# Four taps of a recurrent branch's convolution moved to ScalarE and GpSimd, and three taps of a 31-tap convolution moved from TensorE to VectorE

## The reference, cut to what matters

```python
h = x @ w_in + b_in                      # 1024 -> 2048 columns
a_val, a_gate, b_gate, b_rec = ...       # four slices of 512 channels
ya = silu(layer_norm(causal_depthwise_conv(a_val * sigmoid(a_gate), conv_w, conv_b), ...))   # 31 taps
r  = causal_depthwise_conv(b_rec, lru_conv_w, lru_conv_b)                                     # 4 taps
gate_r = sigmoid(r @ w_a + b_a)          # block-diagonal products
gate_i = sigmoid(r @ w_x + b_x)
a  = exp(-8 * gate_r * softplus(-lam))
u  = sqrt(1 - a*a) * (gate_i * r)
yb = scan(h = a*h + u) * gelu(b_gate)
y  = concat([ya, yb]) @ w_out
```

## Time and profile before

| | |
|---|---|
| median of 3 runs | 3682.91 us (3682.41 to 3684.94) |
| the profiled execution | 3684.21 us, span 3682.3 us |
| busy over the whole span | PE 96%, PEld 77%, DVE 49%, ACT 33%, POOL 15% |
| the stage of the change | from the start to about 260 us |

### The profile page before, as it was taken

How to read it: one execution, slowest core, us unless ns; L and a number is a source line. 1 busy time by engine, 2 the same in 40 slices (tenths; PEclk the granted TensorE clock), 3 DMA queues, 4 the chain that set the end, 5 groups by cost and what they waited for, 6 DMA issues and landing times. The chain is left out here.

```text
span 3682.3 us, 41723 instructions
## 1 busy us (share of the span) xinstructions
PE 3540.3 (96%) x16052; PEld 2841.6 (77%) x16052; DVE 1788.0 (49%) x2304; ACT 1225.3 (33%) x1791; POOL 537.3 (15%) x304
## 2 busy tenths in 40 slices
PE   8989999999998999999999999999987799999997
PEld 6757888888876777767888888888876678888886
DVE  7986423223245666667423233554565674323235
ACT  4244411111134444455311112445353442212133
POOL 0015200000043000013100000445022630000004
PEclk9999999999999999999999999999987899999998
DMA  2002213122122111112222122222220122111112
GB/s 103 34 35 75 92 63 108 46 76 90 45 75 86 47 40 46 40 58 75 87 74 91 46 97 102 93 92 94 91 89 32 70 86 95 48 46 51 45 58 98
DMA packets 77471, 259.07 MB, mean 70 GB/s; under 512 B 10288, under 2 KB 11696, under 8 KB 77360
## 3 DMA queue, kind: packets, MB, share of 16 engines
q1 hardware_dynamic: 77360, 257.59, 20.8%
HBM read 244.45 MB, written 4.72 MB: 68 GB/s over the span
## 5 line engine op out<-in xcount | busy, mean ns | idle before, releaser
L202 PE MATMUL ps<-xh,whi 128*128 128x512 f32 x2768 | 964.6, 395 | 41.8 <-DVE wlo L185 18.1
L202 PE MATMUL ps<-xl,whi 128*128 128x512 f32 x2768 | 957.1, 392 | 0.0
L202 PE MATMUL ps<-xh,wlo 128*128 128x512 f32 x2768 | 956.3, 391 | 0.0
L185 DVE TENSOR_TENSOR wlo<-stage,whi 128x1024 fp32r<-128x1024 f32 (+1 forms) x361 | 505.6, 1401 | 481.3 <-ACT whi L178 480.2
L178 ACT ACTIVATE whi<-stage 128x1024 fp32r<-128x1024 f32 (+1 forms) x361 | 377.7, 1046 | 1031.8 <-PE ps L202 1003.5
L202 PEld LDWEIGHTS ps<-xh,whi 128*128 128x128 f32 x2768 | 524.1, 189 | 159.9 <-issue 28.8
L202 PEld LDWEIGHTS ps<-xh,wlo 128*128 128x128 f32 x2768 | 524.0, 189 | 110.4
L202 PEld LDWEIGHTS ps<-xl,whi 128*128 128x128 f32 x2768 | 524.2, 189 | 107.7
L202 PE MATMUL ps<-hh,whi 128*128 128x512 f32 x1216 | 422.5, 396 | 5.9 <-ACT lam_t L2272 3.9
L202 PE MATMUL ps<-hl,whi 128*128 128x512 f32 x1216 | 421.4, 395 | 0.0
L202 PE MATMUL ps<-hh,wlo 128*128 128x512 f32 x1216 | 421.1, 395 | 0.0
(11 more groups left out here) (411 smaller groups left out, 3933.1 us busy)
## 6 DMA issues: line engine op xcount, KB each, us to landing
stage<-in_w_ff SPq DMA_DIRECT2D x88, 512.0 KB, 3.4
stage<-in_w_gate SPq DMA_DIRECT2D x59, 512.0 KB, 3.2
stage<-in_w_up SPq DMA_DIRECT2D x59, 512.0 KB, 3.2
stage<-in_w_in SPq DMA_DIRECT2D x50, 512.0 KB, 3.2
ada<-in_w_ada SPq DMA_DIRECT2D x48, 512.0 KB, 3.3
stage<-in_w_qkv SPq DMA_DIRECT2D x43, 512.0 KB, 3.2
stage<-in_w_down SPq DMA_DIRECT2D x48, 448.0 KB, 3.3
stage<-in_w_out SPq DMA_DIRECT2D x24, 512.0 KB, 3.2
```

The source lines that it names most:

```text
L185: dve.tensor_tensor(wlo[slot][:, n], stage[slot][:, n], whi[slot][:, n].bitcast(F32), ALU.subtract).then_inc(w_split, 1)
L202: done = pe.matmul(acc[:, h * HALF:(h + 1) * HALF], wt[slot][:, w], xt[:, b, h * HALF:(h + 1) * HALF], start=b == 0 and wt is whi and xt i ...
```

## The change

PE_TAPS falls from 6 to 3, so DVE has 28 (in the last block 20) convolution taps to do instead of 25 (17). The recurrent branch's four taps leave DVE. ACT now writes the four products into rec, g_i, g_r and gel (L662 of the changed kernel), which are free at that time, and POOL adds them: rec+g_i, g_r+gel, and, after a wait for both, rec+g_r. PE waits for the last of these before the gate products. ACT waits for the first two additions before it overwrites gel with the gelu.

```diff
-    PE_TAPS, LATE_TAPS = 6, 8
+    PE_TAPS, LATE_TAPS = 3, 8
...
+    LRU_STEPS = 2 * LRU_TAPS - 1
+    lru_parts = (rec, g_i, g_r, gel)
...
         def _(pool):
             pool.memset(w_gates[:], 0.0).then_inc(wg_zero, 1)
+            for i in range(AB):
+                pool.wait_ge(lru_taps, LRU_STEPS * i + LRU_TAPS)
+                pool.tensor_tensor(rec[:], rec[:], g_i[:], ALU.add).then_inc(lru_taps, 1)
+                pool.tensor_tensor(g_r[:], g_r[:], gel[:], ALU.add).then_inc(lru_taps, 1)
+                pool.wait_ge(lru_taps, LRU_STEPS * i + LRU_TAPS + 2)
+                pool.tensor_tensor(rec[:], rec[:], g_r[:], ALU.add).then_inc(lru_taps, 1)
...
-                pe.wait_ge(lru_taps, LRU_TAPS * i + LRU_TAPS)
+                pe.wait_ge(lru_taps, LRU_STEPS * i + LRU_STEPS)
...
                     act.wait_ge(tap_mm, i + 1)
                     diagonals(i + 1, CONV_TAPS - PE_TAPS, PE_TAPS, diag)
+                act.wait_ge(acc_free, u + 5)
+                for t, part in enumerate(lru_parts):
+                    act.activation(part[:], r_pad[:, t:t + S], ACT.Identity, scale=col("lru_w", LRU_TAPS * i + t),
+                                   bias=col("lru_b", i) if t == 0 else 0.0).then_inc(lru_taps, 1)
+                act.wait_ge(lru_taps, LRU_STEPS * i + LRU_TAPS + 2)
                 act.wait_ge(mm_done, u + 6)
...
-                for t in range(LRU_TAPS):
-                    lru_tap(t)
-                    conv_steps(1)
                 conv_steps(min(SPLIT_AT, n_taps + 1) - step[0])
```

More of the change, by code:

```diff
@@ L717, in conv_steps @@
                         step[0] += 1
[L719 to L725, removed]
                 dve.wait_ge(mm_done, u + 4)
```

## The result

The changed kernel takes 3689.46 us (median of 20 runs) against 3685.18 us of the kernel before (20 runs beside it): a ratio of 1.0016, 95% interval 1.001 to 1.0022. By the bound of 0.2% that is no change, but the interval leaves out 1.000: it is slower, by 4.3 us between the two medians and by 5.9 us by the ratio. The forecast was a change of +0.8 us.

A forecast was written before the change was run, and what follows sets the result against it. PE was taken to set the pace, DVE's own cycle only 3.6 us under it. Three DVE-bound periods (+3.2 us) and the last block (-2.4 us) summed to +0.8 us, 3683.7 us on the median; range 3675 to 3692.

The forecast's parts named there:

- The main case: Loop blocks: POOL's additions and DVE's two-SBUF-input steps exclude each other, DVE sets a 58.35 us period; chance 0.62.
- r_pad without a wait: DVE, loop blocks: r_pad follows a_pad's group without waiting, since DVE comes 1.4 us behind unit 2's end.
- The third rival: Loop blocks: each addition holds DVE 2.35 us or more, step 14 not among them; +7.2 us, 3690.1 us; chance 0.13.
- PE's saving: PE, loop block: 12 of 24 tap matmuls go, at 0.413 us each, saving 5.0 us.
- ACT's products, no table load: ACT, behind the diagonals: four 128x1024 products take 4.0 us with no table load ahead; POOL starts at 10.7 us.
- The exclusion: DVE beside POOL's three additions: 2.16 us lost each, less 1.1 us for step 14 reading PSUM, 5.4 us a loop block.
- the strict rule: The skill's version: a two-SBUF-input DVE instruction and an SBUF-reading POOL one block fully, 2.35 us per addition, 7.05 a block.
- Then 3.03 and units 0 and 1 (22.05) bring it to 45.1: PE, loop block: after rec at 20 us, gate products and units 0 and 1 end 45.1 us after unit 2's end.
- the half clock that "is hidden": PE, units 0 and 1: 3 us at half clock cost 1.5 us, hidden by 0.8 us until wlo and 1.4 until DVE.
- The last block: Last block: a_t comes 27.9 us after r_pad instead of 30.29, giving back 2.4 us.
- Rec at 17.2 and the gates done by 20.7: Last block, PE: rec ready 17.2 us and gate products done by 20.7 us after unit 2's end.
- The rival "POOL starved": Loop blocks: DVE always gets in first, POOL runs only beside step 14 or DVE's waits; +21 us, 3704 us; chance 0.06.

The follow-up runs named there:

- filler: The changed kernel with four unused float32 matmuls (eight records, 3.4 us) into ps[3] ahead of PE's wait for rec: 3684.58 us, ratio 1.0000.

## Why the prediction was right, and where a term was off

The range held the time and "no change" by 0.2% was the likeliest case, but the forecast was +0.8 us and the profile shows +5.1. The main case was right on what the additions do to DVE and wrong on who sets the period; that "no change" held is owed to the 7.4 us that it allows, and so in part to luck. (Of the 5.8 us between the forecast of 3683.7 and the median of 3689.46, 2.3 are the kernel before, whose median was 3682.91 over 3 runs and 3685.18 over 20.) Of its own signs two failed, r_pad without a wait (it waits 0.90 to 2.17 us) and periods near 58.3, and the first addition, 3.77 us, lay above the 3.5 named. The third rival's 3690.1 us is nearest to the time, but its mechanism, DVE held up for 2.35 us or more by each addition outside the PSUM step, is not what the rows show. By its own steps:

- *PE's saving.* The taps row shrank from 10.47 to 5.32 us, 5.15 us for the 5.0 of the forecast: right.
- *ACT's products, no table load.* From 51.33 to the last one's end at 55.69, 4.4 us against 4.0, no load ahead of them; the additions start 10.8 us after unit 2's end (55.77 - 44.97), forecast 10.7.
- *The exclusion.* Three steps held up by 1.03, 2.09 and 2.09 us, 5.2 us against 5.4, with L727 untouched among them. The kernel with the partial sum one step earlier has DVE's cycle bare: 57.9 to 58.0, forecast 58.35. The first and the strict rule were near each other here: 2.09 measured, 2.16 from rows, 2.35 for the whole length; the measured loss is less than the strict rule gives. In the last block three steps lose 6.4 us, forecast 6.5.
- *"Then 3.03 and units 0 and 1 (22.05) bring it to 45.1", and the half clock that "is hidden".* This step failed. Rec was ready at 66.12 - 45.0 = 21.1 us after unit 2's end instead of 20, because DVE's next step went ahead of the first addition; the wait was 5.0 us instead of 3.8. And the half clock was taken too small: the forecast had 3 us at half clock, a loss of 1.5 us; in the three blocks the gate products took 2.3, 1.5 and 2.8 us longer. In block 0 that is 3.5 us together, where PE had 0.8 us in hand until wlo and 1.4 us until DVE, so that the period became PE's. Over three blocks the sum was +6.7 us (178.55 - 171.83) instead of +3.2. With 1.2 us less of wait the same hiding holds, as the kernel with the step earlier shows; with filler, too, where the clock held.
- *The last block.* "Rec at 17.2 and the gates done by 20.7" failed by a wait that I had not put in the sum: PE's gate products overwrite ps[2], and all three additions had been put ahead of step 14, which I had used for DVE's cost but not for PE. L727 was done at 243.36, 19.7 us after unit 2's end, though rec was ready at about 17.5, forecast 17.2. The gate products then took 1.8 us longer at half clock, which the sum for this block had left out too, so that ACT's chain ended 2.83 us after DVE was there. The term was +0.4 us instead of -2.4.
- The rest: r_pad of block 0 came 0.8 us earlier than before, and 1.2 us were given back behind the stage. 6.7 + 0.4 - 0.8 - 1.2 = +5.1. Neither of the last two was forecast, and nothing shows that the change made them: over all the runs here that r_pad starts anywhere from 45.2 to 47.4 us.

The rival "POOL starved" was rejected on rows in which DVE's instructions came when POOL already had its turn. It is real: it took one step in each looped block of the changed kernel, and five in one block of an experiment.

## What to carry to other kernels

An addition of two SBUF tensors on POOL next to a busy DVE is no free work: it took 2.35 us of its own and 2.1 us of DVE's time, where DVE does the same in 1.2. Move to POOL what only writes, or what falls where DVE reads PSUM or waits, and put a PSUM-reading step on DVE where POOL has to get in. When two engines' cycles are within a few us, shift work until they meet, not as much as can be moved. Here one, two or three of six taps by themselves gave 0.22 to 0.26%, which these runs can't tell apart, and the detour over ACT and POOL turned that into a loss. In such a sum count for every wait of PE its length and the half clock behind it, and every reason of the wait, the reuse of its output buffer too; a wait of 5 us lost 1.5 to 2.8 us more by the clock.

## What the runs showed of the hardware that was not expected

A POOL instruction with SBUF inputs can be kept out by a DVE that issues two-input steps without a gap. A single-column addition, 0.18 us by itself, took 5.04 us until DVE came to its PSUM-reading step; this is POOL in the kernel of one-column additions, last block:

```profile
210.74 5.04 POOL L570 TENSOR_TENSOR rec<-rec,g_i 128x1 f32<-128x1 f32 x1 [47.09 <-ACT gel L662]
215.73 0.18 POOL L571 TENSOR_TENSOR g_r<-g_r,gel 128x1 f32<-128x1 f32 x1
```

In the last block of the kernel with filler a full addition took 6.89 us in the same way. With PE's six taps kept, the first addition took 4.82 us and ended 2.3 us after DVE's last step of that run (64.08 + 1.2), the next two, with DVE idle, 2.33 and 2.34. In other blocks (2.5 to 3.6 us) it got in behind the step that was running. What decides between the two was not found. The moment of its issue within DVE's step (one starts every 1.195 us) does not sort the cases simply: where a two-input step came next, additions issued 0.0, 0.7 and 1.04 us behind a step's start got in ahead of it, and those issued 0.25 to 0.55, 0.98 and 1.08 to 1.18 us behind it were kept out. Once one full addition had got in, the next ones took turns with DVE, step by step, as long as DVE had steps to do.
